# Seven half-size products in place of eight in the mixing and second feed-forward product of a two-layer decoder, with the weights' differences made on GpSimd and VectorE

## The reference, cut to what matters

```
u     = h @ w_in                                # heads, gates, values
mixed = concat(retention, pooling, attention)   # 528 x 1024
h     = layer_norm(h * alpha + mixed @ w_out)            # the mixing product
ff    = silu(h @ w_ffn1) * (h @ w_ffn3)                  # 528 x 2816
h     = layer_norm(h * alpha + ff @ w_ffn2)              # the second feed-forward product
```

## Time and profile before

| what | us |
|---|---|
| median of three timed runs (3250.01 to 3260.01) | 3254.3 |
| the profiled execution: span from the first to the last instruction | 3252.7 |
| of it the two decoder layers, from about 1735 us on | 1517.7 |

### The profile page before, as it was taken

The page is one execution under the profiler, slowest core; times in us unless marked ns, Lnnn a source line. Parts: engine busy times, 40 slices in busy tenths (PEclk is TensorE's granted clock), DMA queues, the critical chain, the costliest instruction groups (busy, mean ns, idle before and its releaser), DMA issues.

```text
span 3252.7 us, 52666 instructions
## 1 busy us (share of the span) xinstructions
PE 3120.2 (96%) x22631; PEld 1747.5 (54%) x22631; DVE 975.8 (30%) x2146; ACT 540.8 (17%) x1129; POOL 47.2 (1%) x58
## 2 busy tenths in 40 slices
PE   9878989999999999999999999999999999999999
PEld 3355545333343333333345668574785758675866
DVE  1633455232223223222363431223023122132101
ACT  1332311111111111111122220130102100040000
POOL 0000002000000000000010000000000000000000
PEclk9888979999999999999989999999999999999999
DMA  9800115999999999999863333234333243243532
GB/s 400 354 1 27 53 53 224 386 410 403 408 397 406 400 406 407 407 407 404 351 251 119 125 130 117 111 143 176 135 126 142 105 194 133 100 176 116 195 145 100
DMA packets 97466, 743.70 MB, mean 229 GB/s; under 512 B 11128, under 2 KB 38336, under 8 KB 57552
## 3 DMA queue, kind: packets, MB, share of 16 engines
q1 hardware_dynamic: 58768, 687.49, 53.6%
q10 hardware_dynamic: 32624, 30.52, 2.9%
q0 software_dynamic: 5968, 24.14, 1.9%
HBM read 674.98 MB, written 67.13 MB: 228 GB/s over the span
## 4 chain that ended last, share of the span: by engine, by line
PE 55%; DMA 28%; DVE 3%; ACT 2%; issue 1%; ACTq 1%; POOL 0%; DVEq 0%
DMA arena<-x_sorted 27%; PE psum L1593 19%; PE psum L1610 9%; PE psum L1540 5%; PE psum L1579 3%; PE psum L1551 3%; PE psum L1244 1%; PE psum L802 1%; ACTq L587 1%; PE psum L1355 1%; PE psum L820 1%; PE psum L1196 1%; PE psum L1319 1%; PE psum L1411 1%; PE psum L1457 1%
## 5 line engine op out<-in xcount | busy, mean ns | idle before, releaser
L1244 PE MATMUL psum<-weight_ring,arena 128*32 128x512 f32 x6192 | 680.8, 594 | 23.6 <-DVE arena L2862 21.7
L1593 PE MATMUL psum<-arena,weight_ring 128*128 128x256 f32 (+1 forms) x2816 | 632.2, 383 | 3.1 <-ACT arena L2226 3.1
L1593 PEld LDWEIGHTS psum<-arena,weight_ring 128*128 128x128 f32 x2816 | 527.6, 189 | 99.0 <-issue 11.0
L1244 PEld LDWEIGHTS psum<-weight_ring,arena 128*32 128x32 f32 x6192 | 199.7, 110 | 485.5 <-issue 464.3
L1319 PE MATMUL psum<-weight_ring,arena 128*32 128x256 f32 x6144 | 338.2, 380 | 0.0
L1610 PE MATMUL psum<-weight_ring 128*128 128x512 f32 x704 | 305.4, 593 | 4.2 <-DVE weight_ring L3149 4.2
L1319 PEld LDWEIGHTS psum<-weight_ring,arena 128*32 128x32 f32 x6144 | 196.6, 110 | 153.0 <-issue 26.8
L1610 PEld LDWEIGHTS psum<-weight_ring 128*128 128x128 f32 x704 | 132.9, 190 | 169.3 <-issue 162.5
L2884 DVE STREAM_TRANSPOSE arena<-arena 128x384 f32<-128x384 f32 x32 | 18.6, 580 | 630.8 <-DMA arena<-x_sorted 630.8
L3149 DVE TENSOR_TENSOR weight_ring<-weight_ring,psum 128x256 f32<-128x256 f32 (+1 forms) x88 | 37.5, 426 | 486.1 <-PE psum L1593 480.3
L1540 PE MATMUL psum<-weight_ring,arena 128*128 128x512 f32 (+2 forms) x512 | 170.0, 489 | 3.1 <-ACT arena L2226 3.1
(11 more groups left out here) (435 smaller groups left out, 2532.0 us busy)
## 6 DMA issues: line engine op xcount, KB each, us to landing
weight_ring<-exp_gu SPq DMA_DIRECT2D x129, 2048.0 KB, 11.9
weight_ring<-weights SPq DMA_DIRECT2D x104, 2048.0 KB, 7.8
weight_ring<-exp_down SPq DMA_DIRECT2D x64, 2048.0 KB, 11.5
x_sorted<-arena SPq DMA_DIRECT2D x2, 10752.0 KB
arena<-x_sorted ACTq DMA_DIRECT2D x132, 96.0 KB, 21.6
y_sorted<-arena ACTq DMA_DIRECT2D x128, 96.0 KB, 17.6
y_sorted<-arena SPq DMA_DIRECT2D x2, 5632.0 KB, 39.7
y_sorted<-arena SPq DMA_DIRECT2D x2, 5120.0 KB, 37.3
```

The source lines that it names most:

```text
L1244: mm = pe.matmul(psum[j * GROUP:(j + 1) * GROUP, g, :], xg[:, k // 4, g, k % 4 * GROUP:(k % 4 + 1) * GROUP], w[:, kk, j * 512:(j + 1) * 51 ...
L1593: mm = pe.matmul(bank[:, 0:b - a], w[:, k, col:col + P], h2_t[:, k, a:b], start=(k == 0), stop=(k == KT - 1))
```

## The change: what it does

Each mixing product and each chunk of the second feed-forward product of two 128-row tiles (there are 16 of them, "units") is taken as a product of 2 x 2 blocks: the two tiles by the two halves of the inner dimension, times the two halves of the inner dimension by the two halves of the columns. It is computed with seven products of blocks instead of eight (the Winograd form of Strassen's method). With A11, A12 the first tile's inner halves, A21, A22 the second tile's, and B11 to B22 the weights' blocks:

The diff, cut to its core:

```diff
-FF_CHUNKS = ((0, 12), (12, FT))
+FF_CHUNKS = ((0, 8), (8, 16), (16, FT))
+LAST_CHUNK = len(FF_CHUNKS) - 1
+FAST_MIX = [(0, "A"), (0, "B"), (1, "A"), (1, "B")]
+FAST_CHUNKS = (0, 1, 2)
+STEP_SLOTS = dict(mix=(), down=(2, 5), up=(0, 2, 4, 6))
...
# TensorE
+            def fast(u, piece, steps, ready, ready_late):
...
+                wa, at_a = weights(l, piece)
+                ready()
+                if has_meta(l, x):
+                    wb, at_b = weights(l, piece + 1)
+                    ready_late(META)
+                    if name == "down":
+                        each(steps)
+                    meta_rows(("fast", u, "meta"), operand, by_halves(at_a), by_halves(at_b), depth)
...
+                product_1()
+                if not has_meta(l, x):
+                    wb, at_b = weights(l, piece + 1)
+                ready_late(P)
+                if turning is None:
+                    step(1)
+                    product_5()
+                    step(2)
+                    product_2()
...
+                bank_6 = main.open(pe, bz)
+                pe.wait_ge(sums_ready, count_at(sums_of, u, "t2"))
...
+                mm = product(bank_6, lambda k: fast_s2[:, k, :], b11)
+                bank_7 = main.open(pe, bx)
+                pe.wait_ge(diffs_ready, 3 * u + 3)
...
+                step(5)
+                pe.wait_ge(sums_ready, count_at(sums_of, u, "v"))
+                mm = product(main.psum[:, by, :], lambda k: fast_s4[:, k, :], b22, False)
+                pe.wait_ge(sums_ready, count_at(sums_of, u, "c22"))
+                mm = product(bank_7, lambda k: rows(depth + k, first), b21, False)
+                piece_free[at_a] = piece_free[at_b] = main.done()
...
# GpSimd
+            def differences(u):
+                if u:
+                    pool.wait_ge(part_filled, 3 * u - 1)
+                    pool.wait_ge(sums_ready, count_at(sums_of, u - 1, "t2"))
+                pool.wait_ge(layer_landed[at_a % LAYER_SLOTS], layer_count(at_a))
+                pool.tensor_tensor(fast_t1[:, 0:depth, :], b12, b11, ALU.subtract).then_inc(diffs_ready, 1)
...
+                for part in (slice(0, depth // 2), slice(depth // 2, depth)):
+                    pool.tensor_tensor(b12[:, part, :], b22[:, part, :], b12[:, part, :], ALU.subtract).then_inc(diffs_ready, 1)
+            for u, key in enumerate(FAST):
+                differences(u)
+                if key in loads:
+                    load_norm(*loads[key])
...
# VectorE
+                if has_meta(l, x):
+                    if name == "down":
+                        each(steps)
+                    meta_added(("fast", u, "meta"), scale)
+                if turning is None and opens_chunk(u):
+                    sums()
...
+                    third_difference()
+                    step(2)
+                    add(t, 0, main.take(dve, ("fast", u, "c11")), scale, main.drained["v"])
+                    if ready is not None:
+                        half_stats(t, 0)
+                fourth_difference()
+                bank = main.take(dve, ("fast", u, "p6"))
+                then(dve.tensor_tensor(fast_u2, fast_u2, bank, ALU.add), main.drained["v"])
+                V.did(dve.tensor_tensor(fast_v, fast_u2, main.peek(("fast", u, "c12")), ALU.add), sums_ready)
+                    add(t, 1, fast_u2, scale)
+                    add(first, 0, fast_u2, scale)
+                    add(first, 1, fast_v, scale)
...
+                dve.wait_ge(part_filled, 3 * u + 3)
+                add(first, 1, main.peek(("fast", u, "c21")), 1.0, sums_ready)
+                if ready is not None:
+                    half_stats(first, 1)
+                step(5)
+                add(t, 1, main.take(dve, ("fast", u, "c12")), 1.0, main.drained["v"])
+                if ready is not None:
+                    half_stats(t, 1)
+                    centered = norm_centered(t)
+                add(first, 0, main.take(dve, ("fast", u, "c21")), 1.0, main.drained["v"])
+                if ready is not None:
+                    norm_scaled(centered, ready, parts)
+                    half_stats(first, 0)
+                    norm_scaled(norm_centered(first), ready, parts)
+                    if has_meta(l, x):
+                        half_stats(0, 0)
+                        half_stats(0, 1)
+                        norm_scaled(norm_centered(0), ready, parts)
```

More of the change, by code:

```diff
@@ L2273, in feed_up, with hidden_copied @@
                     A.did(act.activation(ff_t[:, f - FF_CHUNKS[c][0], 0:b - a], bank[:, 0:b - a], ACT.Silu), main.drained["a"])
+            def hidden_copied(u, tile):
+                name, l, x, i = FAST[u]
+                at = OFF[WHOLE[x][tile == "first"]] - span(l, x)[0]
+                f = 4 * i - FF_CHUNKS[[c for c in range(len(UP_UNITS)) if i in UP_UNITS[c]][0]][0]
+                bank = main.take(act, ("turned", u, tile))
+                A.did(act.copy(ff_t[:, f:f + 4, at:at + P], bank.rearrange("p (k s) -> p k s", k=4)), main.drained["a"])
@@ L2306, in layers @@
                 each(steps, PLANS["B"].steps)
+                mix(0, "B")
                 roots(3)
@@ L2316, in layers @@
                 steps = attend(1, "B")
-                feed_up(1, "A", 0, steps)
-                feed_down(1, "A", 0, steps)
-                feed_up(1, "A", 1, steps)
+                for c in range(LAST_CHUNK):
+                    feed_up(1, "A", c, steps)
+                    feed_down(1, "A", c, steps)
+                feed_up(1, "A", LAST_CHUNK, steps)
                 each(steps, PLANS["B"].steps)
+                mix(1, "B")
                 roots(3, 4)
-                last = feed_down(1, "A", 1, none, True)
+                last = feed_down(1, "A", LAST_CHUNK, none, True)
                 turn_rows("mid", 1, "B", (last,))
@@ new lines, in add, with meta_added @@
+            def add(tile, half, other, factor, done=None):
+                part = h2[:, tile, half * 512:(half + 1) * 512]
+                V.did(dve.scalar_tensor_tensor(part, part, factor, other, ALU.mult, ALU.add), done)
+            def meta_added(key, factor):
+                bank = main.take(dve, key)
+                for j in range(4):
+                    part = h2[0:META, 0, j * 256:(j + 1) * 256]
+                    V.did(dve.scalar_tensor_tensor(part, part, factor, bank[32 * j:32 * j + META, 0:256], ALU.mult, ALU.add),
+                          main.drained["v"] if j == 3 else None)
```

525 lines of the change are left out of this document (400 added, 125 removed).

## The result

In timed runs side by side (20 of each kernel) the kernel after takes 3261.2 us and the kernel before 3254.3: ratio **1.0021, interval 1.0011 to 1.0030**. That is 7 us slower, inside the 0.3% that the prediction called no change, where it had forecast 15 us faster. The profiled execution's span is 3263.9 us, 11.2 more than before's; 5.1 of that lies ahead of the layers, whose start moves between 1729.5 and 1748.9 us from one profiled execution to the next, so the layers are compared by themselves.

The account below looks back on a forecast made before the run. TensorE, busy 96% of 3252.7 us, bounds the kernel. Saving 51.5 us of matmuls against 36.6 of new waits gives -14.9: 3237.8, or 3239.4 on the median's scale; range 3219 to 3258.

Parts of the forecast that it names:

- the 120 instructions: In the mixing products and second feed-forward, four runs together need 120 fewer matmul instructions at 0.429 us: 51.5 us saved.
- the norm ahead of the next unit's S1: Where a unit follows a layer norm, TensorE waits for VectorE's first sum or GpSimd's difference: +7.8, +3.6, +7.2 us.
- turned rows: Turning the rows of (1,B): ScalarE's copies of the second tile stand behind the norm's later root, +2.2 us.
- end: Behind the last matmul: the first tile's scaling now stands there too and VectorE is 0.4 late, +2.0 us.
- The value 3.2 for T1: GpSimd's first difference, 1536 columns in the last feed_down of (1,A), takes 3.2 us, reading its two inputs in turn.
- The clock: Behind four stalls of about 3 us or more TensorE's clock drops, 3.0 us each: +12 (ends +6 and +17).
- inside one unit: Nothing stalls in a plain unit; with attention steps VectorE is just in time, apart from one short wait: +1.5 us.
- the last rival: The change saves no matmul time because its products run slower than 429 ns an instruction; chance 0.02.
- The rival of exclusion: GpSimd's differences and VectorE's two-input operations block each other in three units around a norm: +10, to 3249 us; chance 0.24.
- contention with the clock's upper end: Upper end of the range, 3258 us: GpSimd and VectorE block each other and the low clock costs its most.
- 0.13 + 0.01 + 0.01: The chance of slower, given as 0.14; the 0.13 is the rival that VectorE becomes the bound, net +25, 3279 us.

Follow-up runs that it names:

- the kernel with one column: Against the change as it is, GpSimd subtracts one column instead of its whole differences (products not right): layers 1497.3 us, ratio 0.9940 to the kernel before.

## Why the prediction was wrong

**Right.** What bounds the kernel, the 120 instructions, and that inside a run of products an instruction still takes 0.43 us. The step "the norm ahead of the next unit's S1" held at all three places within 0.7 us (8.50, 4.27 and 7.80 for 7.8, 3.6 and 7.2), with the releasers named; turned rows and end held within 0.6. The value 3.2 for T1 was near the measured 3.44. The Trainium skill's page "GPSIMD Engine Reference" (section 3.1) has 4497 ns for an add of 2048 columns; the trace agrees, with 4518 for a subtraction, and by the 3.4 that the prediction estimated from it the sum would have been 0.2 nearer.

**The clock.** Predicted 12 at four places, measured 10.5 there. Windows of the kernel after around mix(0,B) (length, busy times, granted clock, DMA share, GB/s):

```profile
2245.00:2247.00 2.00, 0.34 (x1) 0.30 (x2) 1.90 (x4) 0.00 (x0) 0.00 (x0) 1.00 0.00 0
2259.00:2261.00 2.00, 0.00 (x0) 0.00 (x0) 1.77 (x2) 0.00 (x0) 0.24 (x1) 0.50 0.97 418
2261.00:2263.00 2.00, 1.56 (x2) 0.84 (x3) 1.93 (x4) 0.00 (x0) 0.32 (x1) 0.50 0.51 205
2263.00:2265.00 2.00, 2.00 (x4) 0.68 (x3) 2.00 (x2) 0.00 (x0) 0.00 (x0) 0.50 0.80 328
2265.00:2267.00 2.00, 2.00 (x5) 0.90 (x4) 0.45 (x1) 0.00 (x0) 0.00 (x0) 0.85 0.00 0
```

Behind 2.81 us of idle time the clock stays at 1.00; behind 8.50 it is at half (1.2 of 2.4 GHz) and comes back in the window from 2265 on. The 0.50 stands in the window before the first matmul too: it fell during the stall.

**Wrong: the step "inside one unit", +1.5.** It priced VectorE's work in a unit from rows in which GpSimd did nothing, and let GpSimd's 145 us of differences cost nothing but their own length on the path. Measured: 15.0 us of waits and 1.7 of clock. With these in place of 1.5 and 0 the prediction's sum is +0.3; the errors of the other terms add 1.2, and the last 4.7 are the clock at the layers' start, by chance (1.7), and the 3 us of busy time at the seams of the products, which the sum put at nothing (the last rival spoke of slower products, at 0.02, but not of seams).

The rival of exclusion was in the text, with the right mechanism, at 0.24 and +10. Both numbers were low for the same reason. It counted two-input operations in the three units around a norm. The traces have two of its places at 2.81 (for 4.4), no stretch over 0.9 us at the third, and four it did not look for: an attention's 16 x 32 addition, TENSOR_SCALARs in a unit with meta rows, an S1 behind a T3 (1.50), and an attention step late in (1,A) (1.27). What no row of before could exclude was given a low chance because no row showed it; but the one text that spoke of it, the Trainium skill's page "SBUF — State Buffer" (section "Who interferes with whom"), stated it without a condition that this kernel lacked. The trace agrees with it: from 1740 us on, 64 operations of VectorE began inside a subtraction of GpSimd. The 37 that read PSUM, or were reductions, statistics or reciprocals, kept their length to 0.01 us. Of the 27 that read SBUF alone and were two-operand operations or TENSOR_SCALARs, 24 took 0.4 us or more longer (the 16 x 32 one lasted until GpSimd's end), and three, which began in the last 0.22 us of the subtraction, 0.1 us or less. By that page and the stalls as worked out, the chance of "no change or slower" should have been the larger.

**The range** ended at 3258, contention with the clock's upper end. The exclusion at its measured size would still have lain inside it: +0.3 is 3254.6 on the scale of the median. What carried the time to 3261.2 are the 1.2 of the other terms, the clock by chance and the seams. So the exclusion accounts for 15 of the 21 us by which the layers missed, and for the lost gain; that the time fell beyond the range took the small terms too. (In the prediction's chances, 0.13 + 0.01 + 0.01 is 0.15 and not 0.14; nothing hangs on it.)

## What to carry to other kernels

Here, work given to GpSimd was free only where VectorE, while it ran, read PSUM or did reductions, statistics or reciprocals; where the two met, even a 16 x 32 addition waited for the end of a GpSimd instruction of 4.5 us. So look at what VectorE has in hand when GpSimd's operands become ready, start GpSimd there late rather than as early as possible, and cut its instructions. When a norm stands ahead of work that TensorE needs, list every engine's queue behind it (here VectorE's sums, ScalarE's copy, GpSimd's difference, the bank's drain, the parameter transfer): moving only the first shows the next at nearly the same length.

## What the runs showed of the hardware beyond what was expected

- GpSimd's subtraction of two SBUF operands takes 1.31 us for 512 columns, 3.44 for 1536 and 4.52 for 2048: about 2.1 ns a column and 0.25 us an instruction.
- Cut into 512 columns, GpSimd and VectorE take turns, one instruction each. Both are slowed: four T1 parts that take 5.13 us in the attention take 6.47 beside VectorE's T4, which takes 2.80 for 1.74.
- A single-operand TENSOR_SCALAR is held up as well as a two-operand addition (an 8-column one took 2.23 us for 0.17); a RECIPROCAL, also from SBUF, is not.
- A parameter transfer of 1 MB that starts with two pieces of 2 MB lands after 12.5 us, and after 5.0 when it starts 4 us ahead of them.
- Neither length nor place alone says whether a stall of about 3 us costs the clock. Of 2.81 us between dense products it stayed at 1.00 in the change as it is; at the same place 2.93 in the kernel with short GpSimd instructions was followed by 0.50. Behind the turned rows it fell after 2.76 us and stayed at 1.00 after 2.77 in the kernel with one column. Every stretch of the layers from 4.03 us on, in all kernels, was followed by 0.50; up to 8.5 us, each took 1.6 to 3.1 us of clock.
